# Expert weights in loads of two megabytes, 16 KB of each in one piece for each partition

## The reference, cut to what matters

```python
def expert_choice_ffn(h, w_router, w_gate, w_up, w_down):
    cap = max(1, EC_FACTOR * s // N_EXPERTS)            # 32
    logits = jnp.einsum('bsd,de->bse', h, w_router).astype(jnp.float32)
    aff = jax.nn.softmax(logits, axis=-1)
    g, idx = lax.top_k(jnp.swapaxes(aff, 1, 2), cap)
    xe = h[bidx, idx]
    a = jnp.einsum('becd,edf->becf', xe, w_gate)        # 1024 -> 2048
    u = jnp.einsum('becd,edf->becf', xe, w_up)          # 1024 -> 2048
    ye = jnp.einsum('becf,efd->becd', jax.nn.silu(a) * u, w_down)   # 2048 -> 1024
    ye = ye * g[..., None].astype(ye.dtype)
    return jnp.zeros_like(h).at[bidx, idx].add(ye)
```

## Time and profile before

| | |
|---|---|
| time, median of 3 runs | 2855.05 us (2854.32 to 2856.69) |
| span of the profiled execution | 2852.6 us |
| TensorE matmul busy | 2446.2 us (86%) |
| TensorE weight load busy | 1693.9 us (59%) |
| VectorE / ScalarE / GpSimd busy | 1238.9 (43%) / 935.4 (33%) / 61.3 us (2%) |
| DMA | 698.11 MB, mean 245 GB/s |
| mean granted TensorE clock | 0.906 of full speed |

### The profile page before, as it was taken

One profiled execution on the slowest core, in us unless ns is written; L12 is line 12 of the kernel. 1 busy time (PEld: TensorE's weight loads), 2 busy tenths in 40 slices (PEclk: granted clock), 3 DMA queues, 4 the chain that ended last, 5 costly groups with the idle time before them and its releaser, 6 DMA issues.

```text
span 2852.6 us, 38351 instructions
## 1 busy us (share of the span) xinstructions
PE 2446.2 (86%) x16680; PEld 1693.9 (59%) x16680; DVE 1238.9 (43%) x1752; ACT 935.4 (33%) x1522; POOL 61.3 (2%) x36
## 2 busy tenths in 40 slices
PE   8999998666666676667889899999999999987998
PEld 8897784111211121111578778889788788977787
DVE  5567552000000000100366665477654656855654
ACT  5556541000000000000254554445444443733442
POOL 0000010000000000000000000000000000032000
PEclk9999999777677677776899999999999999999999
DMA  7553478999999999999624255565655554412552
GB/s 240 167 157 117 141 266 342 418 417 416 418 418 418 417 416 417 418 418 418 240 91 132 89 172 194 181 225 173 207 185 195 183 190 148 153 61 77 169 195 94
DMA packets 309927, 698.11 MB, mean 245 GB/s; under 512 B 35424, under 2 KB 211808, under 8 KB 275072
## 3 DMA queue, kind: packets, MB, share of 16 engines
q1 hardware_dynamic: 307456, 681.78, 64.4%
q0 software_dynamic: 2016, 13.67, 1.3%
q10 hardware_dynamic: 288, 0.22, 0.0%
HBM read 694.58 MB, written 1.05 MB: 244 GB/s over the span
## 4 chain that ended last, share of the span: by engine, by line
PE 60%; DMA 29%; DVE 7%; ACT 3%; issue 1%; SPq 0%; DVEq 0%; ACTq 0%
PE ps L565 16%; PE ps L567 16%; PE ps L566 16%; DMA af<-in_w_exp_gate 12%; DMA af<-in_w_exp_up 10%; DMA af<-in_w_exp_down 7%; PE ps L1621 2%; PE ps L2392 1%; PE ps L1652 1%; PE ps L1143 1%; DVE ar L538 1%; PE ps L858 1%; PE ps L2012 1%; PE ps L990 1%; PE ps L1156 1%
## 5 line engine op out<-in xcount | busy, mean ns | idle before, releaser
L565 PE MATMUL ps<-ar 128*128 128x512 f32 (+1 forms) x2688 | 939.8, 350 | 29.0 <-DVE ar L1973 7.0
L567 PE MATMUL ps<-ar 128*128 128x512 f32 (+1 forms) x2688 | 922.0, 343 | 0.0
L566 PE MATMUL ps<-ar 128*128 128x512 f32 (+1 forms) x2688 | 921.7, 343 | 0.0
L538 DVE TENSOR_TENSOR ar<-af,ar 128x1024 fp32r<-128x1024 f32 x520 | 612.0, 1227 | 291.3 <-ACT ar L527 291.1
L565 PEld LDWEIGHTS ps<-ar 128*128 128x128 f32 x2688 | 513.9, 191 | 108.6 <-issue 12.3
L527 ACT ACTIVATE ar<-af 128x1024 fp32r<-128x1024 f32 x520 | 516.3, 1049 | 154.3 <-PE ps L567 152.8
L567 PEld LDWEIGHTS ps<-ar 128*128 128x128 f32 x2688 | 513.8, 191 | 58.7
L566 PEld LDWEIGHTS ps<-ar 128*128 128x128 f32 x2688 | 514.4, 191 | 55.5 <-issue 0.5
L1621 PE MATMUL ps<-af 128*32 128x512 f32 x2048 | 370.6, 821 | 185.0 <-DMA af<-in_w_exp_up 93.6
L1621 PEld LDWEIGHTS ps<-af 128*32 128x32 f32 x2048 | 50.6, 125 | 488.3 <-DMA af<-in_w_exp_up 239.8
L1652 PE MATMUL ps<-af 128*32 128x512 f32 x1024 | 178.9, 815 | 92.9 <-DMA af<-in_w_exp_down 78.9
(11 more groups left out here) (284 smaller groups left out, 1647.0 us busy)
## 6 DMA issues: line engine op xcount, KB each, us to landing
af<-in_w_exp_gate SPq DMA_DIRECT2D x128, 1024.0 KB, 25.4
af<-in_w_exp_up SPq DMA_DIRECT2D x128, 1024.0 KB, 24.9
af<-in_w_exp_down SPq DMA_DIRECT2D x128, 1024.0 KB, 21.4
af<-in_ffn_w_in SPq DMA_DIRECT2D x88, 1024.0 KB, 5.7
af<-in_ffn_w_out SPq DMA_DIRECT2D x44, 1024.0 KB, 5.2
af<-in_w_in SPq DMA_DIRECT2D x33, 1024.0 KB, 5.2
af<-in_sgu_w_in SPq DMA_DIRECT2D x16, 1024.0 KB, 6.8
af<-in_w_out SPq DMA_DIRECT2D x12, 1024.0 KB, 5.3
```

The costliest lines, as they stand in the source:

```text
L538: e.tensor_tensor(self.WL[load.pair][:, c], self.base(i)[:, c], f_(self.WH[load.pair][:, c]), ALU.subtract).then_inc(*self.dve.inc(("lo", ...
L565: e.matmul(o, lh, rh, start=start, stop=False, skip_group_check=True)
L566: e.matmul(o, lh, rl, start=False, stop=False, skip_group_check=True)
L567: return e.matmul(o, ll, rh, start=False, stop=stop, skip_group_check=True)
```

## The change

The expert weights come in loads of 2 MB. A gate or up load takes 256 rows, and partition p gets rows 2p and 2p+1 of them, which lie behind one another in memory: one piece of 16 KB. A down load takes 512 rows, partition p gets rows 4p to 4p+3, again one piece of 16 KB. An expert has 8 gate and up loads and 4 down loads; all have 192 in place of 384. The places are nine slots of four units (numbers 4 to 12) in place of eighteen of two, which together hold 18 MB as before. Slots 7 and 8 lie over the small slots 0 and 1, and 2 and 3. `load.before` becomes a tuple, since a load may have to wait for two. `AHEAD` is 2 (4 MB in place of 6). To free whole groups of four units, the scratch of the expert stage moves from `B(6)` to `B(4)` and `H2T` from `B(2)` to units 44 and 45.

Since the rows lie otherwise over the partitions, the other operand is picked to match: the gather reads its stationary operand at every second element, and the transpose of the product reads at every fourth element. The matmuls on the weights are the same in number and shape; eight in a row now go to one accumulator bank.

```diff
-PARTS = (0, 16, 32, 47)
-SLOT_UNIT = {0: 32, 1: 34, 2: 36, 3: 38, 4: 0, 5: 2, 6: 4, 7: 6, 8: 8, 9: 10, 10: 40, 11: 42, 12: 44, 13: 20,
-             14: 26, 15: 28, 16: 14, 17: 30}
-EXPERT_SLOTS = (8, 9, 10, 11, 12, 13, 14, 0, 1, 2, 3, 6, 7, 4, 5, 15, 17, 16)
-AHEAD = 6
+PARTS = (0, 18, 32, 47)
+SLOT_UNIT = {0: 32, 1: 34, 2: 36, 3: 38, 4: 8, 5: 40, 6: 24, 7: 32, 8: 36, 9: 0, 10: 4, 11: 28, 12: 14}
+EXPERT_SLOTS = (4, 5, 6, 7, 8, 9, 10, 11, 12)
+AHEAD = 2
...
-            load.before = in_slot.get(load.slot)
-            in_slot[load.slot] = q
...
+            under = {7: (0, 1), 8: (2, 3), 0: (7,), 1: (7,), 2: (8,), 3: (8,)}.get(load.slot, ())
+            load.before = tuple(sorted(in_slot[t] for t in ((load.slot,) if free.get(load.slot) else under) if t in in_slot))
...
-            for k in range(8):
+            for k in range(4):
                 for n in ("w_exp_gate", "w_exp_up"):
-                    add([(lambda s: s, A[n][x, k * P:(k + 1) * P, :])])
+                    add([(lambda s: s, A[n][x, 2 * k * P:(2 * k + 2) * P, :].rearrange("(p j) n -> p (j n)", j=2))])
...
-            for k in range(0, 16, 2):
-                add([(lambda s: k_(s, 2), rows(A["w_exp_down"][x])[:, k:k + 2, :])])
+            for k in range(4):
+                add([(lambda s: s, A["w_exp_down"][x, 4 * k * P:(4 * k + 4) * P, :].rearrange("(p j) n -> p (j n)", j=4))])
...
         if slot in EXPERT_SLOTS[0:AHEAD]:
             return self.over("xo_in")
-        if slot == 14:
-            return [self.pool.val(("sum", "xa_o", 1, 1))]
+        if slot == 6:
+            return [self.pe.val(("over", "merged")), self.pool.val(("sum", "xa_o", 1, 1))]
...
-        if slot == 16:
-            return [self.pe.val(("ps", "h2", 1, 1))]
+        if slot == 12:
+            return [*self.over("mix"), self.pe.val(("ps", "h2", 1, 1))]
...
-                        t = e.matmul(ps[:, b, i * P:(i + 1) * P], self.H2T[:, tt, d * P:(d + 1) * P],
+                        t = e.matmul(ps[:, b, i * P:(i + 1) * P], self.H2T[:, tt, :].rearrange("p (k q j) -> p k j q", k=4, j=2)[:, d // 2, d % 2, :],
...
-                t = e.transpose(ps[:, b, i * P:(i + 1) * P], S1[:, i * P:(i + 1) * P], self.IDN)
+                t = e.transpose(ps[:, b, i * P:(i + 1) * P], S1.rearrange("p (q j) -> p j q", j=4)[:, i, :], self.IDN)
```

More of the change, by code:

```diff
@@ L302, in plan @@
         count, pairs, in_slot, in_pair, ring = [0], [0], {}, {}, [0, 1]
+        free, landed = {}, {}
         def add(parts, n=0):
@@ L307, in add @@
             count[0] += 1
-            load.before = in_slot.get(load.slot)
-            in_slot[load.slot] = q
-            before = self.loads[load.before].value[1] if load.before is not None else 0
-            load.value = (self.landed[load.slot], before + 16 * len(parts))
+            under = {7: (0, 1), 8: (2, 3), 0: (7,), 1: (7,), 2: (8,), 3: (8,)}.get(load.slot, ())
+            load.before = tuple(sorted(in_slot[t] for t in ((load.slot,) if free.get(load.slot) else under) if t in in_slot))
+            for t in under:
+                free[t] = False
+            free[load.slot], in_slot[load.slot] = True, q
+            landed[load.slot] = landed.get(load.slot, 0) + 16 * len(parts)
+            load.value = (self.landed[load.slot], landed[load.slot])
             if n:
@@ L420, in plan @@
         out, ahead = self.at["out"], self.at["gate_up", 0]
-        mixed = [q for i in range(AHEAD) for q in ([out + i] if i < 4 else []) + [ahead + i]]
+        mixed = [q for i in range(4) for q in [out + i] + ([ahead + i] if i < AHEAD else [])]
         self.order = [*range(out), *mixed, *range(ahead + AHEAD, len(self.loads))]
@@ L427, in slot_opens @@
             return self.over("xo_in")
-        if slot == 14:
-            return [self.pool.val(("sum", "xa_o", 1, 1))]
-        if 4 <= slot < 8:
-            last, = (q for q in (self.at["out"] + 2, self.at["out"] + 3) if self.loads[q].pair == (slot - 4) // 2)
+        if slot == 6:
+            return [self.pe.val(("over", "merged")), self.pool.val(("sum", "xa_o", 1, 1))]
+        if slot in (9, 10):
+            last, = (q for q in (self.at["out"] + 2, self.at["out"] + 3) if self.loads[q].pair == slot - 9)
             return [self.pe.val(("used", last, 1))]
-        if slot == 16:
-            return [self.pe.val(("ps", "h2", 1, 1))]
+        if slot == 12:
+            return [*self.over("mix"), self.pe.val(("ps", "h2", 1, 1))]
         return self.over("mix")
     def base(self, q):
-        return self.U_(SLOT_UNIT[self.loads[q].slot], 2)
+        slot = self.loads[q].slot
+        return self.U_(SLOT_UNIT[slot], 4 if slot in EXPERT_SLOTS else 2)
     def pair_w(self, q):
@@ L482, in sync @@
                 e.dma_start(self.WR, A["w_router"].rearrange("(k p) n -> p k n", p=P)).then_inc(*self.router_in.one())
-            if load.before is not None:
-                b = load.before
+            for b in load.before:
                 if self.loads[b].n:
@@ L490, in sync @@
                         e.wait_ge(*w)
-            elif load.slot >= 4:
+            if not load.before and load.slot >= 4:
                 for w in S.new(*self.slot_opens(load.slot)):
@@ L1271, in t_mix @@
             run(self.t_fm(e, "out", c, self.at["out"] + c, both(self.mgp, F), self.halves("merged"), OUT, self.by_dve("out"),
-                          (lambda: self.t_rms(e, "ffn", self.B(6), Ring(4), range(6), last=False)) if c == 3 else None))
+                          (lambda: self.t_rms(e, "ffn", self.B(4), Ring(4), range(6), last=False)) if c == 3 else None))
         self.end(self.pe, "mix")
@@ L1379, in a_mix @@
         merged_hi((2, 3))
-        run(self.a_proj(e, "out", 4, self.a_squares_of("ffn", self.x, self.B(6))))
+        run(self.a_proj(e, "out", 4, self.a_squares_of("ffn", self.x, self.B(4))))
         self.end(act, "mix")
@@ L1615, in t_moe @@
             q, c, XE = self.at["gate_up", x], 32 * (x % 4), self.XE[:, x // 4 % 2]
-            for k in range(8):
+            for k2 in range(4):
                 for bb in (ba, bu):
[L1618 to L1622, removed]
+                    for k in (2 * k2, 2 * k2 + 1):
+                        for j in range(4):
+                            for w in self.Tw.new(self.loads[q].value, dve.val(("xe", x // 4, 0)), act.val(("xe", x // 4, 1)), *free):
+                                e.wait_ge(*w)
+                            o = k % 2 * BIG + 512 * j
+                            t = e.matmul(ps[32 * j:32 * j + 32, bb, :], XE[:, k, c:c + 32], self.base(q)[:, o:o + 512],
+                                         start=k == 0, stop=k == 7)
                     t.then_inc(*pe.inc(("raw", q), *([("ps", "gate_up", x)] if k == 7 and bb == bu else [])))
@@ L1652, in t_moe @@
                         t = e.matmul(ps[o:o + 32, b, :], self.AT_[x % 2][:, r * P + 32 * j:r * P + 32 * j + 32],
-                                     k_(self.base(q), 2)[:, kk, 512 * c:512 * c + 512], start=i == 0, stop=i == 7)
-                t.then_inc(*pe.inc(("raw", q), *([("ps", "y", x)] if i == 7 else [])))
+                                     k_(self.base(q), 4)[:, r, 512 * c:512 * c + 512], start=j == 0 and r < 2, stop=j == 3 and r > 1)
+                t.then_inc(*pe.inc(("raw", q), *([("ps", "y", x)] if j == 3 else [])))
                 q += 1
```

25 lines of the change are left out of this document (12 added, 13 removed).

## The result

| | before | changed |
|---|---|---|
| time, median of 4 runs each | 2854.69 us (2851.04 to 2856.69) | 2835.69 us (2830.24 to 2839.27) |
| ratio, 95% interval | | 0.9926 [0.9914, 0.9938] |
| span of the profiled execution | 2852.6 us | 2832.2 us |
| mean granted TensorE clock | 0.906 | 0.933 |

The changed kernel is 19.0 us faster by the medians, 20.4 by the profiled spans. 19.7 had been forecast.

A forecast was written before the change was run, and what follows sets the result against it. Expert stage bound by DMA, all else by TensorE. Saving 21.6 us from larger pieces, less 0.9 at the start and 1.0 at the end, gives 19.7: span 2832.9, plus 2.45, 2835.3 us; range 2828 to 2852.

The forecast's parts named there:

- What bounds the stage: Expert stage: DMA sets its time, 925.5 us at 416 GB/s; nothing TensorE saves there gives any time.
- The cost of a piece: Expert loads: each further piece costs an engine 8.7 ns; pieces of 16 KB give 427 GB/s and save 21.6 us.
- Nothing for the number of loads: Expert loads: the fixed part of a load is hidden behind queued transfers, so halving their number counts nothing.
- The start, +0.9: Start of the expert stage: the first place needs 8 records more before it is freed, 0.9 us later DMA stream.
- The end, +1.0: End of the expert stage: 16 records instead of 8 after the last landing, +1.0 us taken, up to +1.9 at low clock.
- Strided operands, nothing: Gather's stationary operand at a step of two: nothing taken, at most 3.8 us once; other gathers and transposes under DMA.
- The order ahead of the stage: Expert loads issued before the stage: sixth to eighth at 432.6, ninth at 446.0, all landing in time; no cost.
- Rival 1: Expert loads: pieces over 8 KB bring no more, only down gains 8.8 us; 2848.2 us, chance 0.16.
- Rival 2: Expert loads: neighbouring partitions reading 16 KB apart meet in memory, rate falls to 408 GB/s; 2877.1 us, chance 0.11.
- Rival 3: Expert stage: TensorE takes over as the bound at 60.6 us for each expert; about 2857 us, chance 0.04.
- The 2.45 us between median and span: Whole kernel: the median of the runs stands 2.45 us above the profiled span, added to the forecast span.

The follow-up runs named there:

- run 3: The changed kernel with the old row layout, gather and transposes: 2 MB loads in nine places, pieces of 8 and 4 KB; 2858.64 us, ratio 1.0009.
- run 1: The kernel before with only the 1 MB down loads in one piece of 8 KB per partition instead of two of 4 KB; 2848.95 us, ratio 0.9974.
- run 5: The kernel before with 1 MB down loads in four pieces of 2 KB per partition instead of two of 4 KB; 2875.31 us, ratio 1.0067.
- run 8: The changed kernel itself, unaltered, timed again against the kernel before; 2833.72 us, ratio 0.9922.
- run 2: The kernel before with gate and up loads taking every second row of 256, 16 KB apart, still 8 KB pieces; 2856.59 us, ratio 0.9997.

## Why the prediction was right, point by point

- **What bounds the stage.** Right: large places without large pieces (run 3) leave the window at 925.7 us, though TensorE is busy for 76 us less in it (549 against 625), and the time follows the DMA window: 8.8 us shorter and 7.4 to 8.2 faster in run 1, 18.6 longer and 19 slower in run 5.
- **The cost of a piece.** Right, and the term that carries the result. It was read from two kinds of load, 8.7 ns from 4 to 8 KB, and extended to 16 KB. The stage's windows give it at three doublings: 18.6 us for 126 x 16 pieces from 2 to 4 KB (run 5 against before), 9.2 ns; 8.8 us for 126 x 8 from 4 to 8 KB (run 1), 8.7 ns; 14.0 us for 183 x 8 from 8 to 16 KB (run 1 against the changed kernel), 9.6 ns. That the cost of one more piece is near 9 ns at each size is shown. What the engine spends it on isn't. In every run it is the source in memory that is split; the place in SBUF is one stretch for each partition. The window fell by 22.8 us (925.5 to 902.7) where 21.6 were forecast; the rate is 428 GB/s, not 427.
- **Nothing for the number of loads.** Right (run 3, and the same number in run 1). Had each load cost a fixed 2.0 us, halving them would have given 366 us, as the prediction worked out from the Trainium skill ("DMA: Bandwidth & Descriptors", section "Anatomy of one DMA"); run 3 halves them and gains nothing. The section gives that figure as a fit for a DMA issued by GpSimd, which the prediction leaves out. The loads here are issued by SyncE and queued behind one another, so the runs say nothing against it where it was measured.
- **The start, +0.9.** Right in size: the first byte on a freed place comes 0.9 us after that of before (458.9 against 458.0 in the two traces). SyncE issues it at 458.05 instead of 457.03; of these 1.02 us 0.16 are TensorE's later beginning, and 0.86 are the 8 more records.
- **The end, +1.0.** Mis-sized in the profiled execution: the 16 records took 2.5 us more than the 8 of before. The prediction had priced the low clock at up to +1.9, which is 8 more records at 1.9 us. But at the low clock all 16 run low, and the 8 of before had run at the full one in 1.1 us. From 1.1 to 3.6 is more. In run 8 it was 0.8. A part came back in the same execution: L1668 took 2.0 us against 3.7 for the same 16 records (L1664) before. That belongs to the clock and not to the change, since L1664 took 2.0 us in run 2 too, which has the old places and loads:

```profile
1386.52 2.00 PE L1664 MATMUL ps<-af 64*128 64x256 f32 x16 [0.72 <-ACT af L1695]
```

- **Strided operands, nothing.** Off by 0.2 us, inside the bounds of 0 to 3.8.
- **The order ahead of the stage.** Right: the sixth to eighth loads went at 432.5 to 433.4, the ninth at 446, and TensorE waited for none of them.
- **Rival 1** (no more above 8 KB) is refuted by the windows at 428. **Rival 2** (spacing) is refuted by run 2, by the 428 GB/s of the changed kernel itself at 16 KB, and by run 1, where down reads 8 KB apart instead of 4. The row of the Trainium skill that the prediction cites for it ("DMA: Bandwidth & Descriptors", section "Latency and other measured facts", row on HBM row pitch) advises contiguous tiles but gives no rate for them; "full rate" is the prediction's reading. **Rival 3** (TensorE takes over) did not come: its busy time in the stage fell.

The sum over the profiled spans: 23.0 for the pieces (first byte to last landing), less 0.9 at the start, less 2.5 at the end, and 1.7 back at L1668, makes 21.3. The first matmul behind the stage (L565, L568 after) began 21.2 us earlier:

```profile
1407.64 0.35 PE L565 MATMUL ps<-ar 128*128 128x256 f32 x1 [0.64 <-ACT ar L880]
```

```profile
1386.40 0.36 PE L568 MATMUL ps<-ar 128*128 128x256 f32 x1 [0.64 <-ACT ar L883]
```

The spans differ by 20.4 us only. The missing 0.8 us were lost somewhere in the rest of the span and were not followed up.

The mechanism was right, and the pieces came within 1.4 us of the forecast. That the total came within 0.4 us of 2835.3 is partly luck: the end cost 1.5 us more than forecast and 0.8 us went astray, and against them stand 1.4 us from the pieces and 1.7 from a clock that the prediction had not reckoned with. The 2.45 us between median and span, which it took over, were 3.5 this time. The four times of the changed kernel alone lie 9 us apart.

## What to carry to other kernels

Where a long stretch runs at the DMA limit, look at windows that hold only one kind of load: two rates at the same bytes per load point to a cost for each contiguous piece, and here it could be carried to piece sizes that no row showed (16 KB in the change, 2 KB in run 5). Make the piece for one partition longer by giving a partition neighbouring rows, and permute the other operand to match; in this kernel that was the whole gain, and large loads and large places added nothing while the DMA engines had work queued. Count what large places cost at both ends, and what all places together hold before the consumer starts: that was all that one place more gave here.

## What the runs showed that was not expected

- With loads of two megabytes TensorE's mean granted clock in the stage was higher: 0.73 before and 0.74 in run 1, with 8 records after each landing; 0.82 in the changed kernel and 0.81 in run 3, with 16. TensorE's busy time in the stage fell from 625 to 553 us. The size of the load isn't the only way to it: run 5, with loads of 1 MB and slower matmuls on them (661 us busy), had 0.79. The higher clock is worth nothing inside the stage. At its end the level at the last landing decides 1.6 us.
- SyncE's issue stalls in some of these kernels. With 18 places of 1 MB only some ten loads were under way, and an issue of SyncE itself took 2 to 4 us; with 2 MB in single pieces it took 0.33 us, and eight loads, 16 MB, were under way. The issues before, in run 1 and in run 3 (min/median/max in ns):

```profile
L496 SPq DMA_DIRECT2D af<-in_w_exp_gate x128: 327/2133/7212, 381.1 to 1331.4; - x128
L496 SPq DMA_DIRECT2D af<-in_w_exp_down x128: 367/4306/5727, 433.9 to 1366.1; - x128
```

```profile
L496 SPq DMA_DIRECT2D af<-in_w_exp_gate x128: 327/2136/7218, 380.9 to 1322.7; - x128
```

```profile
L499 SPq DMA_DIRECT2D af<-in_w_exp_gate x64: 367/4616/10669, 380.7 to 1326.2; - x64
af<-in_w_exp_gate SPq DMA_DIRECT2D x64, 2048.0 KB, 28.7
```

  Run 3 stalls with 28.7 / 4.98, about six loads or 12 MB, under way, and the changed kernel doesn't with eight loads or 17 MB. So neither the number of loads nor their bytes sets the stall. The number of pieces would fit. As estimates from the median times to landing, an engine has 87 pieces under way in run 1 (27.2 / 2.49 x 8) and 92 in run 3 (28.7 / 4.98 x 16), against 67 in the changed kernel (41.3 / 4.93 x 8). No run set out to test that. In none of these kernels did the DMA engines run dry, so the stalls cost nothing here.

- A stationary operand of float32 read at a step of two elements took 4.01 us for 32 records in the changed kernel and in run 2, against 3.81 before and in runs 1 and 3.
